# The chain of small operations for the forget gates, three turns later in VectorE's order

## The reference

```python
h = rms_norm(x, norm1_g[l]) * (1.0 + sc1) + sh1
(fq, fk, fv, ff, nq, kc, vc, ksl, vsl, kwn, vwn, ng, ca, cg) = split_in(h @ w_in[l])
log_f = jax.nn.log_sigmoid(ff.astype(jnp.float32) + b_f[l].astype(jnp.float32))
o_fox = fox_attention(hd(fq), hd(fk), hd(fv), log_f)      # logits += F[t] - F[s], F = cumsum(log_f)
...
o_conv = conformer_conv(ca, cg, conv_w[l], conv_b[l], conv_ln_g[l], conv_ln_b[l])   # 31 taps
mixed = jnp.concatenate([o_fox, o_nsa, o_conv], axis=-1)
x = x + g1 * (mixed @ w_out[l])
...
x = x + g2 * (jnp.square(jax.nn.relu(h @ w_mlp1[l])) @ w_mlp2[l])
```

## Time and profile before

| | |
|---|---|
| median of 3 runs | 1179.87 us (1176.31 to 1180.24) |
| the profiled execution, its own time | 1177.99 us |
| its span from the first to the last instruction | 1175.9 us |
| TensorE matmuls | 1137.2 us busy (97%) |
| VectorE | 983.7 us busy (84%) |
| ScalarE | 641.4 us busy (55%) |
| mean granted TensorE clock | 0.986 of full speed |
| the moved chain | 14 instructions, 196.03 to 199.1 us |

### The profile page before, as it was taken

The page is one execution under the profiler, slowest core; times in us unless marked ns, Lnnn a source line. Parts: engine busy times, 40 slices in busy tenths (PEclk is TensorE's granted clock), DMA queues, the critical chain, the costliest instruction groups (busy, mean ns, idle before and its releaser), DMA issues.

```text
span 1175.9 us, 17828 instructions
## 1 busy us (share of the span) xinstructions
PE 1137.2 (97%) x7081; PEld 1008.9 (86%) x7081; DVE 983.7 (84%) x1182; ACT 641.4 (55%) x936; POOL 23.5 (2%) x40
## 2 busy tenths in 40 slices
PE   4999999999999998999999999999999999999996
PEld 4899989998887777999788888888888888888885
DVE  5998989888987988996887788987788987878774
ACT  6655458876775556544544445554445544445452
POOL 1000000100000000010000000000000000000000
PEclk7999999999999999999999999999999999999998
DMA  9999998978956898995556675557675657666451
GB/s 378 419 419 421 422 402 306 258 200 299 342 215 221 304 316 302 390 349 189 190 210 252 249 268 197 206 188 268 239 280 179 215 195 271 250 224 265 154 179 72
DMA packets 48322, 314.65 MB, mean 268 GB/s; under 512 B 6572, under 2 KB 8440, under 8 KB 11768
## 3 DMA queue, kind: packets, MB, share of 16 engines
q1 hardware_dynamic: 44592, 305.72, 70.0%
q0 software_dynamic: 1760, 5.26, 2.4%
q10 hardware_dynamic: 1896, 2.64, 0.8%
HBM read 305.20 MB, written 4.21 MB: 263 GB/s over the span
## 4 chain that ended last, share of the span: by engine, by line
PE 78%; DVE 10%; DMA 5%; ACT 4%; issue 3%; SPq 0%; ACTq 0%; DVEq 0%
PE quad L1275 15%; PE quad L1289 10%; PE quad L1291 10%; PE quad L1290 10%; PE quad L1277 8%; PE quad L1265 5%; PE quad L1266 5%; PE quad L1267 5%; DMA first_raw<-in_w_mod 3%; DVE w_lo L1821 2%; PE quad L1336 2%; PE quad L1337 2%; PE quad L1335 2%; DMA mod_raw<-in_w_mod 2%; DVE first_raw L1828 2%
## 5 line engine op out<-in xcount | busy, mean ns | idle before, releaser
L883 ACT ACTIVATE w_hi<-raw 128x1024 fp32r<-128x1024 f32 (+1 forms) x342 | 355.4, 1044 | 311.4 <-PE quad L1291 116.2
L1821 DVE TENSOR_TENSOR w_lo<-raw,w_hi 128x1024 fp32r<-128x1024 f32 (+1 forms) x342 | 408.6, 1205 | 113.6 <-ACT w_hi L883 112.0
L1275 PE MATMUL quad<-act,w_hi 128*128 128x512 f32 x768 | 266.4, 391 | 0.0
L1265 PE MATMUL quad<-act,w_hi 128*128 128x256 f32 x760 | 216.2, 285 | 6.6 <-DVE w_lo L1821 4.4
L1277 PE MATMUL quad<-act,w_lo 128*128 128x256 f32 x768 | 216.8, 282 | 0.0
L1266 PE MATMUL quad<-act,w_hi 128*128 128x256 f32 x760 | 213.9, 281 | 0.0
L1267 PE MATMUL quad<-act,w_lo 128*128 128x256 f32 x760 | 213.5, 281 | 0.0
L1275 PEld LDWEIGHTS quad<-act,w_hi 128*128 128x128 f32 x768 | 144.2, 188 | 29.9
L1265 PEld LDWEIGHTS quad<-act,w_hi 128*128 128x128 f32 x760 | 144.5, 190 | 9.6 <-issue 5.3
L1289 PE MATMUL quad<-w_hi,u_hi 128*128 128x512 f32 x376 | 149.0, 396 | 0.6 <-DVE u_lo L2278 0.6
L1291 PE MATMUL quad<-w_hi,u_lo 128*128 128x512 f32 x376 | 148.9, 396 | 0.0
(11 more groups left out here) (368 smaller groups left out, 1719.5 us busy)
## 6 DMA issues: line engine op xcount, KB each, us to landing
raw<-in_w_main SPq DMA_DIRECT2D x184, 1024.0 KB, 5.0
mod_raw<-in_w_mod SPq DMA_DIRECT2D x68, 1024.0 KB, 7.0
first_raw<-in_w_mod SPq DMA_DIRECT2D x14, 1024.0 KB, 15.6
late_raw<-in_w_mod SPq DMA_DIRECT2D x10, 1024.0 KB, 8.4
acc<-in_w_mod SPq DMA_DIRECT2D x4, 1024.0 KB, 12.3
conv_b<-conv_q POOLq DMA_DIRECT2D x8, 512.0 KB, 5.2
x_a<-in_x SPq DMA_DIRECT2D x2, 1024.0 KB, 7.2
x_scratch<-x SPq DMA_DIRECT2D x1, 2048.0 KB, 12.8
```

What stands on the lines that cost most here:

```text
L883: A(dst[:, 0:2 * width], block_half(raw, j, width), ACT.Copy).then_inc(hi_done, 1)
L1265: mm(out, hi, act_hi[:, k, :], start=begin and m % 2 == 0, stop=False, skip_group_check=True)
L1275: mm(out, w_hi[j % 4][:, cols], act_both[:, k, :, :].rearrange("p h t -> p (h t)"), start=begin, stop=False, skip_group_check=True)
L1821: TTn(lo[:, 0:2 * width], block_half(raw, j, width), hi[:, 0:2 * width].bitcast(f32), ALU.subtract)\
```

## The change

The 14 operations move from turn 60 to turn 63 of VectorE's order. There they stand behind the `w_lo` of half 63 and the sum of a tap, and ahead of the `w_lo` of half 64. The first two operations of the gates (turn 58), ScalarE's exponential (turn 59) and TensorE's use of the result (slot 64) stay where they are. No instruction is added or taken away, and no DMA issue is moved.

```diff
-                if turn == LF_TURN + 2:
+                if turn == LF_TURN + 5:
 
 
                     e, r, r2, s = (lf[i][:, :, :] for i in (1, 2, 3, 4))
```

## The result

The changed kernel takes 1182.3 us (median of 7 runs, 1180.89 to 1183.59) against 1179.57 us before (7 runs): a ratio of 1.003, 95% interval [1.002, 1.0041]. (The ratio is taken over all the runs; that of the two medians is 1.0023.) It is 2.7 us **slower**; forecast were 1.6 us less, and 1182.3 lies above the range of 1174.8 to 1181.0. By the bound of 0.5% it is still "the same", the likeliest of the three classes, but the loss is clear of the scatter. The profiled execution took 1180.89 us, its span is 1178.9 us.

The account below looks back on a forecast made before the run. TensorE, busy 97% of the span, was taken as the bound, so only its standing still could be won. Removing the 1.64 us wait before half 61, with nothing added late, gave 1179.87 - 1.64 = 1178.2 us, range 1174.8 to 1181.0.

Parts of the forecast that it names:

- The wait at 199.9: TensorE before half 61: standing idle for a late w_lo 61, which the move takes away, winning at most 1.64 us.
- The chain's price of 3.03 us: VectorE, turn 63: the same 14 operations cost the same 3.03 us in the new place, holding back w_lo 64.
- the forget sums cover w_lo 64: TensorE, slot 64: forget sums take 1.5 us, so half 64 starts at 209.9, 2.0 us after its w_lo is ready.
- The sum as a whole: Whole kernel: median 1179.87 less 1.64 gives 1178.2 us, -0.14%; chance 0.60.
- What the change adds: Engines walked on after the move: nothing late, smallest margin 1.2 us; loads going out sooner costed at nothing.
- the margin of 1.2 us: VectorE to TensorE at half 68: w_lo 68 ready at 219.9, wanted at 221.1; the smallest margin, before it was 3.3.
- one thing can pin it: First attention scores: ScalarE's wait for a GpSimd transfer could hold VectorE until 234.0, losing 0.4 us.
- I take the full 1.6 us: From slot 72 on: the whole gain goes through to the end; bounds of this term 1.2 and 1.64 us.
- What is left of it later: After 201.5 us: TensorE's gain reaches slot 72, and VectorE's first scores move with it, keeping 1.6 us.
- rival 1: Attention stretch: the saving is given back there, gain 0 us, 1179.9 us; chance 0.11.
- rivals 2 and 3: Attention stretch: a lowered-clock stretch goes (-3.3 us, 1176.5) or one comes on top (+0.1 us, 1179.9); chance 0.11 each.
- Rival 4: TensorE, slot 64: forget sums wait for lf_ok in the old wait's place, slower; 5 us late costs +1.6 us; chance 0.05.

Follow-up runs that it names:

- e8: Changed kernel with a second buffer for the products of taps 8 and 14, no load delayed: median 1177.17 us, ratio 0.9988 [0.9976, 1.0000].
- e10: Changed kernel with a second buffer for the products of taps 8 and 14, and block 34's weight load one half later: 1176.84 us, ratio 0.9986.
- e1: Changed kernel with the weight load of block 34 issued one half later, after w_lo 62: ratio 1.0005 [0.9996, 1.0014] against the kernel before.
- e4: Changed kernel with the weight loads of blocks 34 and 37 each issued one half later: ratio 1.0001 [0.9989, 1.0013] against the kernel before.
- e9: Kernel before, chain in turn 60, with a second buffer for the products of taps 8 and 14: ratio 1.0001 [0.9990, 1.0012].
- e3: Kernel before, chain in its old place, with GpSimd's transfer of tap 5 held until w_lo 61 is written: ratio 1.0053 [1.0037, 1.0070].
- e7: Kernel before with the weight load of block 37 issued one half later: ratio 0.9999 [0.9987, 1.0011].
- e5: Changed kernel, block 34's load one half later, ScalarE held before tap 8's product until half 63 is done: ratio 1.0030 against the kernel before.
- e6: Kernel before without 13 of the chain's 14 operations, nothing moved: median 1181.4 us, ratio 1.0023 [1.0013, 1.0032].

## Why the prediction was wrong

**What held.** The wait at 199.9 and its price of 1.64 us: TensorE's forget sums began at 208.30 (worked out: 208.4). The chain's price of 3.03 us in the new place (203.47 to 206.49: 3.02), the 0.7 to 0.8 us of VectorE's idle time, and that the forget sums cover w_lo 64. The sum as a whole, -0.14%, is met by the medians of e8 and e10 (-0.12% and -0.14%) but not by those of e1 and e4 (+0.05% and +0.01%), in which ScalarE's wait before tap 8 is gone as well.

**The step that failed** is the last point of "What the change adds": "the loads that wait for lo_done between halves 61 and 63 go out 2 to 3 us sooner [...]. VectorE and ScalarE waited for no weight load there, so I cost them at nothing." The issue times were right. (One detail was not: no load waits for w_lo 64. The one that went out later waits for w_lo 65, 211.80 against 210.51.) But I asked only who waits for the loads, not what else is on the DMA engines when a load starts 3 us sooner. The answer stood in the trace: GpSimd's transfer was issued at 198.14 and took 4.8 us, and ScalarE's next DMA tap wanted it landed at 205.14 at the latest. Its slack was 205.14 - 198.14 - 4.8 = 2.2 us, and with ScalarE's own wait of 1.26 us gone, ScalarE was ready for tap 8's product at 203.7 already, and the slack was 0.9 us; the 1 MB load ahead of the transfer cost 5.0.

**What that cost, by steps.** ScalarE +4.14 us. VectorE's w_lo 68 was ready at 222.1 and not at 219.9, so the margin of 1.2 us that was worked out turned into TensorE's wait of 1.07 us. The transfer of tap 11, with a load 0.6 us ahead of it, took 8.6 us and made ScalarE wait 2.94 us (before: 7.5 and 1.09), which kept ScalarE late. At slot 72, TensorE was 0.5 us ahead of the kernel before (0.3 without the 0.16 us by which this whole execution lies ahead) and not 1.64, VectorE 2.4 us behind it: the point "one thing can pin it" named the right place and the right engine, but took the transfers to move with ScalarE. Up to L1546 (305.7 against 304.7) the changed kernel lost another 1.5 us; TensorE's waits for exponentials were 1.7 us longer there. From there to 377.2 (first L1561; before: 374.6) it lost 1.6 us more, all of it by the clock: 0.79 and 0.64 in 340 to 346 and 346 to 352, where the kernel before had 0.76 and 0.96, which is 1.7 us.

**A second step that the runs don't bear out** is "I take the full 1.6 us" in "What is left of it later". Executions lie up to 0.5 us apart from the start on, so I count from the issue of tap 5's transfer. In e1, e4, e8 and e10, without ScalarE's wait before tap 8, TensorE reached slot 72 1.6 us sooner than in the kernel before, as worked out. But VectorE came to the first scores only 0.2, 0.7 and 0.5 us sooner in e1, e4 and e8 and 0.5 us later in e10, where 1.6 us was taken and 1.2 was the lower bound. And in the profiled executions of the kernel before, e8 and e9 the clocks are lowered alike (0.93 in 265 to 290, 0.91 in 335 to 355, 0.94 in 440 to 470), and L1546 comes, by the same count, at 304.7, 304.1 and 304.8, the end at 1175.9, 1175.6 and 1175.9 us. So in these most of TensorE's lead in e8 is given back in the attention stretch, as rival 1 has it. That the medians of e8 and e10 meet the sum may be luck in part.

**The rivals.** None of the five has the mechanism that failed. Rival 1 (given back in the attention stretch) fits what the profiled executions of e8 and e9 show. What rivals 2 and 3 describe both happened in the profiled execution of the changed kernel: the lowered stretch at 276 went, one at 242 came, and the one at 342 became longer. Rival 4, the only slow one, was wrong: no wait for lf_ok came up in any run.

**What stays open.** How much of the median loss is the clock's. The lowered stretch behind 340 us was worth 3.4 us in the profiled executions of the changed kernel, e1, e3 and e7, and 1.6 us in all the others, e5 and e6 among them, whose medians show the loss of the changed kernel or nearly; so it isn't tied to the change. Which waits tip the clock wasn't tried. For the same reason single executions scatter by 2 us either way (e10's profiled one took 1180.68 us, its median is 1176.84), and only the medians carry the verdicts. Where e8 and e10 win what their medians show, and why e1 and e4 don't, stays open too. ScalarE's leftover waits for transfers don't sort them (4.1 and 2.6 us in e1 and e4, 2.2 and 3.3 us in e8 and e10), nor do VectorE's first scores, which are earliest in e4; and the intervals of e4 and e8 overlap.

## What to carry to other kernels

When an engine gets ahead, list every transfer that its semaphores release and lay it over the transfers that are on the way in that moment: a load that nobody waits for can delay one that somebody does. A single buffer between an engine and a slow transfer turned a late transfer into a stall of the engine, and with it of all that stands behind in its order; a second buffer took the whole loss away here. And the test for "this work is in the way" is to leave it out: here that made the kernel slower, which no count of busy time would have told. Before a lowered clock is put down as a cost, look whether the kernel before had one elsewhere: here it had, and the two cancelled.

## What the runs showed of the hardware

The 512 KB transfer of GpSimd's queue, followed 0.26 us later by a 1 MB load of SyncE's queue, didn't share the DMA engines with it: its first packets moved 5.2 us after its issue and not 1.5, and it landed after 9.8 us instead of 4.8. With the load 0.6 us ahead it took 8.3 us (e3), with the load 2.5 us behind 5.5 us (e1). In e1 the first packets of the transfer moved 1.4 us after its issue, in e3 those of the load 0.9 us after its own.

A wait of TensorE of the same length, for the same exponentials, was followed by a lowered clock in one execution (1.87 us before the change, then 0.72 in 276 to 282) and by none in another (1.86 us after the change, 1.00).
